# Attention logits in one VectorE instruction per 128 rows: scale, mask, sink and row extreme together, and an exponential that negates

## The reference

```python
logits = einsum('bqhd,bqkhd->bhqk', qb, kg) * (HEAD_DIM ** -0.5)
logits = where(valid, logits, -inf)          # first block: selected keys only
p = softmax(logits, axis=-1)
...
s = einsum('bnqhgd,bnkhd->bnhgqk', qb, kb) * (d ** -0.5)
# window attention of the second part: keys further than 128 positions away are masked, and each head's
# learned sink is one more logit: it is in the row maximum and in the sum, and has no value row
```

## Time and profile before

| | |
|---|---|
| time, median of 3 runs | 1392.83 us (1391.02 to 1399.88) |
| profiled execution | 1391.93 us, span 1390.2 us |
| TensorE busy | 1238.2 us, 89% of the span |
| VectorE busy | 513.0 us, 37% |
| ScalarE busy | 633.7 us, 46% |
| GpSimd busy | 780.2 us, 56% |
| granted TensorE clock, mean | 0.977 of full speed |

### The profile page before, as it was taken

The page is one execution under the profiler, slowest core; times in us unless marked ns, Lnnn a source line. Parts: engine busy times, 40 slices in busy tenths (PEclk is TensorE's granted clock), DMA queues, the critical chain, the costliest instruction groups (busy, mean ns, idle before and its releaser), DMA issues.

```text
span 1390.2 us, 19388 instructions
## 1 busy us (share of the span) xinstructions
PE 1238.2 (89%) x7815; PEld 1020.7 (73%) x7815; DVE 513.0 (37%) x1008; ACT 633.7 (46%) x1085; POOL 780.2 (56%) x347
## 2 busy tenths in 40 slices
PE   5999999897766766897989999999999889799997
PEld 4878877775322322676778999988998777799986
DVE  3828752543112111344742222202357381322211
ACT  4444534644010110544545655546699442655551
POOL 4779986340000000784008888878778904788884
PEclk9999999998999999898999999999999999899999
DMA  6555554285999999463005555455544422455551
GB/s 233 152 182 181 181 182 151 79 315 227 393 421 418 410 422 415 148 212 106 32 1 174 190 183 182 167 182 182 182 147 157 164 94 93 150 182 182 182 183 75
DMA packets 126047, 275.05 MB, mean 198 GB/s; under 512 B 7380, under 2 KB 53772, under 8 KB 113676
## 3 DMA queue, kind: packets, MB, share of 16 engines
q1 hardware_dynamic: 125692, 272.87, 54.1%
q10 hardware_dynamic: 272, 1.05, 0.2%
HBM read 272.85 MB, written 1.05 MB: 197 GB/s over the span
## 4 chain that ended last, share of the span: by engine, by line
PE 71%; DMA 9%; ACT 7%; DVE 6%; POOL 3%; issue 2%; SPq 1%; ACTq 0%; DVEq 0%
PE lin_ps L867 11%; PE lin_ps L869 11%; PE lin_ps L868 11%; PE lin_ps L887 8%; PE lin_ps L889 8%; PE lin_ps L890 8%; DMA work<-in_w_expert_out 4%; DMA ring<-in_w_expert_in 4%; POOL w_low L798 3%; PE sc_ps L1125 3%; ACT w_high L1390 2%; PE sc_ps L941 2%; PE lin_ps L972 1%; PE lin_ps L1140 1%; PE lin_ps L1112 1%
## 5 line engine op out<-in xcount | busy, mean ns | idle before, releaser
L798 POOL TENSOR_TENSOR w_low<-ring,w_high 128x1024 fp32r<-128x1024 f32 (+1 forms) x320 | 771.5, 2447 | 593.3 <-ACT w_high L1390 593.3
L1390 ACT ACTIVATE w_high<-ring 128x1024 fp32r<-128x1024 f32 (+1 forms) x320 | 311.9, 1040 | 137.6 <-PE lin_ps L869 90.3
L887 PE MATMUL lin_ps<-x_high,w_high 128*128 128x256 f32 x960 | 273.0, 284 | 0.0
L889 PE MATMUL lin_ps<-x_high,w_low 128*128 128x256 f32 x960 | 272.0, 283 | 0.0
L890 PE MATMUL lin_ps<-x_low,w_high 128*128 128x256 f32 x736 | 208.6, 283 | 0.0
L887 PEld LDWEIGHTS lin_ps<-x_high,w_high 128*128 128x128 f32 x960 | 183.4, 191 | 0.1
L889 PEld LDWEIGHTS lin_ps<-x_high,w_low 128*128 128x128 f32 x960 | 183.4, 191 | 0.1
L867 PE MATMUL lin_ps<-w_high,x_high 128*128 128x512 f32 (+1 forms) x432 | 170.5, 395 | 2.9 <-POOL w_low L798 2.6
L868 PE MATMUL lin_ps<-w_low,x_high 128*128 128x512 f32 (+1 forms) x432 | 168.3, 390 | 0.0
L869 PE MATMUL lin_ps<-w_high,x_low 128*128 128x512 f32 (+1 forms) x368 | 143.3, 389 | 0.0
L890 PEld LDWEIGHTS lin_ps<-x_low,w_high 128*128 128x128 f32 x736 | 140.4, 191 | 0.0
(11 more groups left out here) (390 smaller groups left out, 1927.3 us busy)
## 6 DMA issues: line engine op xcount, KB each, us to landing
ring<-in_w_expert_in SPq DMA_DIRECT2D x32, 2048.0 KB, 15.2
ring<-in_ffn_w_in SPq DMA_DIRECT2D x44, 1024.0 KB, 7.7
ring<-in_w_in SPq DMA_DIRECT2D x15, 2048.0 KB, 7.9
ring<-in_b_w_in SPq DMA_DIRECT2D x11, 2048.0 KB, 7.9
work<-in_w_expert_out SPq DMA_DIRECT2D x8, 2048.0 KB, 25.8
ring<-in_w_expert_out SPq DMA_DIRECT2D x8, 2048.0 KB, 21.2
ring<-in_ffn_w_out SPq DMA_DIRECT2D x8, 2048.0 KB, 8.0
ring<-in_w_mem_kv SPq DMA_DIRECT2D x4, 2048.0 KB, 10.7
```

The costliest lines, as they stand in the source:

```text
L798: pool.tensor_tensor(w_low[:, slot, 0:words], raw, w_high[:, slot, 0:words].bitcast(F32), ALU.subtract).then_inc(low_made, 1)
L887: pe.matmul(out, wh[:, j, at], high(k), start=(k == 0 and f < 2), stop=False, skip_group_check=True)
L889: pe.matmul(out, wl[:, j, at], high(k), start=False, stop=False, skip_group_check=True)
L1390: act.activation(w_high[:, slot, 0:words], raw, ACT.Copy).then_inc(high_made, 1)
```

## The change

VectorE's `top` no longer makes a 128x512 logit pass and a reduction. Where there is a mask it issues, for each 128 rows, one `tensor_tensor_reduce` on 128x256: out = (scores + mask) * (-scale), and beside it the minimum of out over the row, started from minus the sink (from 3e38 where there is no sink). So `z_buf` holds negated logits, `nmax` the minimum of them (which is minus the maximum), and ScalarE's exponential gets scale -1. Without a mask (`attx0`, `attx1`) it is still one pass and one reduction, with the scale's sign and max turned into min. A small instruction ahead of `att0` makes `minus_sink`. The mask is now added before scaling, not after.

```diff
@@ program
+FAR_UP = 3.0e38
...
+        minus_sink = sb("minus_sink", [P, ATT_HEADS])
@@ ScalarE, probs
-                        ins = act.activation(p_buf[:, g % 2, t, :], z_buf[:, g % 2, t, :], ACT.Exp,
+                        ins = act.activation(p_buf[:, g % 2, t, :], z_buf[:, g % 2, t, :], ACT.Exp, scale=-1.0,
                                              bias=nmax[:, g % 4, t:t + 1], accum_out=rsum[:, g % 4, t:t + 1])
@@ VectorE, top
                     if mask is None:
-                        ins = dve.tensor_scalar(z_buf[:, g % 2], s, scale, None, ALU.mult)
-                    else:
-                        ins = dve.scalar_tensor_tensor(z_buf[:, g % 2], s, scale, mask, ALU.mult, ALU.add)
+                        dve.tensor_scalar(z_buf[:, g % 2], s, -scale, None, ALU.mult).then_inc(att_z, 1)
+                        dve.wait_ge(att_z, g + 1)
+                        dve.tensor_reduce(nmax[:, g % 4, :], z_buf[:, g % 2], AX, ALU.min).then_inc(att_max, 1)
+                        return
+                    for t in range(TILES):
+                        lowest = minus_sink[:, i:i + 1] if with_sink else FAR_UP
+                        ins = dve.tensor_tensor_reduce(z_buf[:, g % 2, t], s[:, t], mask[:, t], -scale, lowest, ALU.add, ALU.min,
+                                                       accum_out=nmax[:, g % 4, t:t + 1])
                     ins.then_inc(att_z, 1)
                     dve.wait_ge(att_z, g + 1)
-                    if not with_sink:
-                        dve.tensor_reduce(nmax[:, g % 4, :], z_buf[:, g % 2], AX, ALU.max, negate=True)\
-                            .then_inc(att_max, 1)
-                    else:
-                        step(dve.tensor_reduce(nmax[:, g % 4, :], z_buf[:, g % 2], AX, ALU.max))
-                        dve.tensor_scalar(nmax[:, g % 4, :], nmax[:, g % 4, :], sink[:, i:i + 1], -1.0, ALU.max,
-                                          ALU.mult).then_inc(att_max, 1)
+                    dve.sem_inc(att_max, 1)
@@ VectorE, before the window attention
+            step(dve.tensor_scalar(minus_sink[:], sink[:], -1.0, None, ALU.mult))
```

## The result

| | before | changed |
|---|---|---|
| median | 1393.73 us (1389.14 to 1399.88, 15 runs) | 1386.08 us (1381.83 to 1392.31, 15 runs) |
| ratio, 95% interval | | 0.995 (0.9933 to 0.9967) |
| profiled execution | 1391.93 us, span 1390.2 | 1392.31 us, span 1390.5 |

The change gains 7.6 us by the medians, 0.5%. The forecast was a gain of 5.2 us from 1392.83, the median of three runs of the kernel before; over 15 runs that median is 1393.73, so 0.9 of the 7.6 us is the starting point. The profiled execution of the changed kernel happens to be the slowest of its 15 runs, so its span says nothing of the gain; its stages do.

A forecast was written before the change was run, and what follows sets the result against it. A two-head dependence loop in the masked attentions, with VectorE's share wholly on it, was the bound. Gains of 1.3, 3.4 and 0.56 us sum to 5.2: 1391.93 to 1386.7, median 1387.6 us; range 1381.5 to 1396.

The forecast's parts named there:

- VectorE's share: Masked attentions, logits' start to first exponential: 1.45 us in `att`, 1.72 in `att0`, wholly on the two-head loop.
- Places on the chain: Logit passes on the chain: three in `att`, six in `att0`; the start of `att0` counted separately, for 0.56 us.
- TensorE's own limit: `att` loop: VectorE's share can shrink by about 0.8 us before TensorE limits; its weight loads idled 0.83 us.
- The price of the pair: Two new instructions with reads per masked head: 1.03 us for 1.45 in `att`, 1.16 for 1.72 in `att0`.
- The hand-over by a separate increment: End of the new pair: 0.04 us wait on the instruction's semaphore, 0.04 more for the increment of `att_max`.
- Rival A: Accumulator reads nearly free, or shrinking also helps heads 2 and 3: 1384.6 us; chance 0.13, shared with D's better case.
- The sum: Gains of 1.3 us in `att`, 3.4 in the `att0` loop and 0.56 at its start: 5.2 us.
- Half rate: New masked-attention instruction at the scan's rate, 691 ns for 128x256, as the skill's two-SBUF-source rule might suggest.
- B: Nothing gained: scan's rate with overlapping reads, or a later stage gives it back; 1392 to 1393 us; 0.18 with another rival.
- C: Slower: new instruction at half rate, each accumulator read held back; 1395.8 us, chance 0.12.
- the edits nobody waits for: Unmasked attentions' sign and min, `minus_sink` (0.2 us if uncovered), mask and PSUM releases up to 0.4 us later: cost nothing.
- D: TensorE's half clock behind `att0`'s start might vanish, 1384.6 us (0.13 with Rival A); gap expected to stay; new drop costs 3.

The follow-up runs named there:

- direct: Changed kernel with the new instruction itself raising the semaphore, without VectorE's wait and separate increment: 1383.48 us, ratio 0.9931 to the kernel before.
- split_unfused: Kernel before with logit pass and reduction each cut into two of 128x256 in the masked attentions, not fused: 1393.47 us, ratio 0.999.
- doubled: Changed kernel with each new instruction issued twice, same result: 1400.64 us, ratio 1.0057 to the kernel before.
- before_look1: The kernel before, unchanged, in one more profiled execution to look at TensorE's clock: 1392.28 us.

## Why the prediction was right

The decisive step was that VectorE's share lies wholly on a loop over two heads. Five kernels with five shares show it (share, period, and their difference):

| | share in `att` | period | difference | share in `att0` | period | difference |
|---|---|---|---|---|---|---|
| direct | 0.81 | 4.50 | 3.69 | 0.93 | 4.80 | 3.87 |
| changed | 0.87 | 4.55 | 3.68 | 0.99 | 4.86 | 3.87 |
| split_unfused | 1.44 | 5.13 | 3.69 | 1.70 | 5.58 | 3.88 |
| before | 1.45 | 5.14 | 3.69 | 1.72 | 5.59 | 3.87 |
| doubled | 1.80 | 5.48 | 3.68 | 2.05 | 5.92 | 3.87 |

1. *Places on the chain.* Three in `att`: 3 x 0.58 = 1.74 us, measured 1.78. Six in the loop of `att0` and one at its start: 7 x 0.73 = 5.1, measured 5.2 between the first two profiles; over all of them the old `att0` took 50.4 to 51.4 us (52.86 in split_unfused) and the new one, not doubled, 44.1 to 46.1. The counts from the earlier trace rows and the waiting time of the earlier trace rows held. The prediction had put TensorE's own limit at the 0.83 us that its weight loads waited; its products were idle for 0.43 us of the period only (4.71 busy of 5.14), and yet the period fell by 0.59, and by 0.64 in `direct`, so the waiting time of the weight loads was the better guide. At the start of `att0`, the first logits now lie 3.72 us ahead of head 2's, before 4.43: the 0.7 us of that step.
2. *The price of the pair.* 1.03 and 1.16 us were forecast, 0.87 and 0.99 measured. This is the mis-sized term. The main instructions were right (414 and 479 ns forecast, 422 and 482 measured); the accumulator read was taken from ScalarE (0.10 us on the stream and 0.19 for the last row), and VectorE's costs 0.02 and 0.08. The hand-over by a separate increment was put at 0.08 and is about 0.10, of which `direct` takes back 0.06. Rival A's free reads, 0.82 us, were nearer in `att` and equally far off in `att0`.
3. *The sum.* 5.2 us forecast; with the measured shares the same sum is 0.58 x 3 + 0.73 x 6 + 0.73 = 6.9 us, against 7.6 and 8.7 by two sets of medians. The 0.7 to 1.8 us on top aren't explained by the sum; runs scatter by that much, and the half clock at the end of `att0` is a candidate.
4. *Half rate,* rivals B and C. No row of 0.69 us and no held read: the instruction that writes its stream and carries a minimum runs at the plain rate. The prediction said that no row shows it either way, but one row of the kernel before bears on it, a plain instruction of this shape with a scalar column and both sources in SBUF:

```profile
L1931 DVE SCALAR_TENSOR_TENSOR attn<-attn,wi 128x256 f32<-128x256 f32 x14 | 6.2, 481 | 0.6 <-ACT attn L1482 0.3
```

It takes 481 ns, where one source in PSUM gives 479. The rule of the Trainium skill that was weighed (Vector Engine (DVE) Microarchitecture Reference, section 7), half throughput with two SBUF sources that aren't bf16, isn't seen there, nor in the new instruction, whose first source lies in PSUM. The new instruction with both sources in SBUF wasn't run.
5. *What the edits nobody waits for cost.* Nothing, as forecast, but one was mis-sized: `minus_sink` took 845 ns, not 0.2 us, while VectorE still waited 3.17 us for the scores behind it. That its length comes from GpSimd, which was at work until 649.9 us in the stretch before, is a guess.
6. *The clock,* D. The gap behind the start of `att0` stayed, as forecast, but half clock doesn't always follow it: in before_look1 the granted clock is 1.00 from 646 to 692 us. A new drop elsewhere, priced at 3 us there, did come up behind `att` in nearly all executions with the short `att`. It costs 1.2 to 1.6 us, it also comes without the change, and whether the change makes it more frequent stays open. That a stretch of half clock might go away at the end of `att0` (2.6 to 3.5 us) wasn't thought of.
7. *The range and the chances.* 1381.5 to 1396 us held 1386.08, and the wide side above wasn't needed. But the forecast proper, a gain of 3.5 to 6.5 us, had got 0.57, and the gain was 7.6 us, or 6.8 from the forecast's own 1392.83: past its end and nearer to rival A's 8.2 us, which had got 0.13. The mechanism was right, the size too small by a third, for the price of the pair and what lies outside both stages.

## What to carry to other kernels

Find the loop of waits first and split it into its parts; if a part stands wholly on it, each 0.1 us of that part is 0.1 us of the period, whatever the engine's busy share says (VectorE was 37% busy here). Walking the logits once with an instruction that also reduces saved 0.58 of 1.45 us per head; cutting it in two without fusing saved nothing. For a gain of half a percent, compare stages and periods in the profiles (periods and `att` repeated to some 0.02 us, `att0` to 2 us, with the clock) rather than single executions, which here scatter by 5 us either way. And profile the same kernel more than once before a stretch of half clock is put down to a change.

## What the runs showed of the hardware that had not been expected

- VectorE's accumulator read starts together with the next instruction of the stream and takes 83 ns; ScalarE's takes 0.19 us, and the next exponential starts 0.10 us after it.
- The same program has stretches at half TensorE clock in some executions and not in others, for instance the kernel before at 264 to 273 us, with a granted clock of 1.00 in two executions and 0.84 in one. Another lies over the end of `att0` and the start of `attx0` in one of its three profiled executions (0.67 over 4 us) and costs 3.5 us. An execution with more of them can be as slow as the kernel before while the two changed stages are 7 us shorter. What decides where they fall stays open.
